# Routed experts walked block by block: one block of 64 slots per pass in place of pairs, tokens gathered once, put-back summed in PSUM, each expert matrix in one 2 MB transfer

## The reference

```python
def hierarchical_moe(h, w_gr, b_gr, w_er, b_er, w_gate, w_up, w_down):
    t = h.reshape(-1, d)                                   # 256 tokens x 1024
    g_sel = argmax(t @ w_gr + b_gr)                        # 1 of 8 groups
    top_v, top_i = top_k((t @ w_er + b_er)[group g_sel], 2)   # 2 of its 8 experts
    weights = g_gate * softmax(top_v)
    eid = g_sel * 8 + top_i                                # 512 assignments to 64 experts
    # the assignments, sorted by expert, are filled into blocks of one expert each
    hid = silu(xblk @ w_gate[e]) * (xblk @ w_up[e])        # 1024 -> 512, twice
    y = hid @ w_down[e]                                    # 512 -> 1024
    out = zeros.at[buf_tok].add(y * buf_w)                 # back to the tokens, weighted
```

## Time and profile before

| | us |
|---|---|
| runs (three) | 2862.37, 2856.97, 2859.93 |
| median | 2859.93 |
| span of the profiled execution (first to last instruction) | 2857.3 |
| median less that span (what lies around it) | 2.6 |
| first expert load issued | 2180.6 |
| last down matmuls of the experts end | about 2845.4 |
| first experts' matmul starts | 2193.45 |

### The profile page before, as it was taken

One profiled execution on the slowest core, in us unless ns is written; L12 is line 12 of the kernel. 1 busy time (PEld: TensorE's weight loads), 2 busy tenths in 40 slices (PEclk: granted clock), 3 DMA queues, 4 the chain that ended last, 5 costly groups with the idle time before them and its releaser, 6 DMA issues. The chain is left out here.

```text
span 2857.3 us, 42442 instructions
## 1 busy us (share of the span) xinstructions
PE 2778.7 (97%) x17857; PEld 2263.3 (79%) x17857; DVE 1517.0 (53%) x2889; ACT 479.1 (17%) x971; POOL 0.2 (0%) x4
## 2 busy tenths in 40 slices
PE   8999899999999999999999999999997999999998
PEld 8998799999988999888988998888895444443443
DVE  7768677687555775544345666466324322222232
ACT  1001410010043101122010022344101100101001
POOL 0000000000000000000000000000000000000000
PEclk9999999999999999999999999999998999999999
DMA  7544144464444553446544444454544999999996
GB/s 234 204 162 148 59 155 170 136 204 166 127 137 131 164 177 119 122 115 151 174 148 147 145 121 121 135 153 126 148 137 192 425 425 428 426 427 426 426 426 290
DMA packets 370397, 594.89 MB, mean 208 GB/s; under 512 B 15777, under 2 KB 327361, under 8 KB 347585
## 3 DMA queue, kind: packets, MB, share of 16 engines
q1 hardware_dynamic: 365440, 588.01, 58.4%
q10 hardware_dynamic: 4800, 4.63, 0.6%
HBM read 591.52 MB, written 1.08 MB: 207 GB/s over the span
## 5 line engine op out<-in xcount | busy, mean ns | idle before, releaser
L3246 PE MATMUL bank<-ring,wk 128*64 128x512 f32 x1408 | 313.6, 598 | 4.8 <-DMA ring<-in_w_expert_gate 4.8
L851 PE MATMUL bank<-hR,ring 128*128 128x128 f32 x2112 | 266.4, 276 | 4.0 <-DVE hR L427 4.0
L3246 PEld LDWEIGHTS bank<-ring,wk 128*64 128x64 f32 x1408 | 100.0, 138 | 211.5 <-issue 211.5
L851 PEld LDWEIGHTS bank<-hR,ring 128*128 128x128 f32 x2112 | 251.7, 193 | 4.9 <-DMA ring<-in_ffn_w_in 2.7
L3343 DVE TENSOR_TENSOR hT<-bank,hT 128x512 f32<-128x512 f32 x92 | 63.6, 691 | 312.5 <-PE bank L3233 310.1
L3272 PE MATMUL bank<-big,wk 128*64 128x512 f32 x352 | 155.8, 595 | 15.1 <-ACT wk L3303 15.1
L1171 PE MATMUL bank<-big,ring 128*128 128x128 f32 x1320 | 159.6, 275 | 0.0
L1171 PEld LDWEIGHTS bank<-big,ring 128*128 128x128 f32 x1320 | 153.5, 192 | 0.1
L740 PE MATMUL bank<-hR,ring 128*128 128x256 f32 x704 | 152.3, 379 | 0.0
L740 PEld LDWEIGHTS bank<-hR,ring 128*128 128x128 f32 x704 | 133.8, 190 | 18.2
L2276 PE MATMUL bank<-big,ring 128*128 128x256 f32 x640 | 141.0, 379 | 1.5 <-ACT big L2840 1.0
(11 more groups left out here) (454 smaller groups left out, 4718.3 us busy)
## 6 DMA issues: line engine op xcount, KB each, us to landing
ring<-in_ffn_w_in SPq DMA_DIRECT2D x88, 1024.0 KB
ring<-in_w_expert_gate SPq DMA_DIRECT2D x44, 2048.0 KB
ring<-in_w_expert_up SPq DMA_DIRECT2D x44, 2048.0 KB
ring<-in_w_in SPq DMA_DIRECT2D x96, 512.0 KB
big<-in_w_expert_down SPq DMA_DIRECT2D x44, 1024.0 KB
ring<-in_ffn_w_out SPq DMA_DIRECT2D x40, 1024.0 KB
ring<-in_w_up SPq DMA_DIRECT2D x22, 1024.0 KB
hR<-in_w_expert_down SPq DMA_DIRECT2D x22, 1024.0 KB
```

Source lines behind the costliest of these rows:

```text
L851: last = nc.tensor.matmul(k.bank[:, 2 * (n % 4) + p // 4, (p % 4) * P:(p % 4 + 1) * P], a[:, c, m * P:(m + 1) * P], b[:, c, :], start=c == ...
L3246: last = nc.tensor.matmul(k.bank[a:a + SLOTS, 2 + n, :], xg[:, c * P + a:c * P + a + SLOTS], self.weights(j, c, KC), start=c == 0, stop=c ...
```

## The change

The loop goes over single blocks and runs exactly as many times as there are blocks. Gate and up of one block now share a PSUM bank and the two column halves of the array; the two halves of the down product's columns do the same. All 512 assignments' tokens are gathered once, ahead of the loop, sorted by expert without gaps (`sorted_rows`, 8 x 576 columns); a block's 64 tokens are a window in it that starts at `k.first[block]`, which ScalarE copies out. The put-back matmuls add into four PSUM banks that hold the residual stream's sum over all blocks (`start=False`); these are cleared once ahead of the loop and added to the residual stream once behind it. Each matrix of a block has one place, `ring` slot 0 (gate), 1 (up) or 2 (down), and comes in one transfer of 2 MB. The residual rows are copied by ScalarE (in `TokenNorm`) and no longer by VectorE. The first constant's row is widened to 512 numbers. The core of the diff:

```diff
+    PIECES = 3
+    GU, TURN, DOWN = 7, (4, 6), 5
+    def arrived(self, eng, n, i):
+        sem, count = self.landing(n)
+        eng.wait_ge(sem, i * 16 + (count + 16))
+    def freed(self, i, n):
+        return i * self.PIECES + (self.u0 + NSLOT + n)
     def sp(self, sp):
         sp.wait_ge(self.route.eid_ready, 1)
+        with sp.Fori(0, self.blocks(sp)) as i:
+            e = sp.value_load(k.eid[0:1, bass.ds(i, 1)], min_val=0, max_val=NEXP - 1)
...
+            for n, w in enumerate((gate, up, down)):
+                sp.wait_ge(k.w_used, self.freed(i, n + 1 - self.PIECES))
+                sp.dma_start(self.piece(n), w).then_inc(self.landing(n)[0], 16)
+    def clear(self, pe):
...
+        for n in range(4):
+            nc.tensor.matmul(k.bank[:, n, :], self.w(self.GW, P), self.w(self.Y, 512), start=True, stop=True, ...)
+    def gather(self, pe):
...
+        for c in range(KC):
+            if c >= 3:
+                pe.wait_ge(self.xs_taken, c - 2)
+            for t in range(T):
+                last = nc.tensor.matmul(k.bank[:, 5 + c % 3, :], k.xn[:, t, c * P:(c + 1) * P], self.w(self.G + t * 512, 512), ...)
+            last.then_inc(self.xs_made, 1)
+    def put(self, pe, final=False):
...
+        for n in range(4):
+            r = slice((n % 2) * SLOTS, (n % 2 + 1) * SLOTS)
+            last = nc.tensor.matmul(k.bank[:, n, :], gw[r, (n // 2) * P:(n // 2 + 1) * P], y[r, :], start=False, stop=True, ...)
     def pe(self, pe):
+        with pe.Fori(0, n) as i:
+            pe.wait_ge(self.xg_ready, i + 1)
+            for m in range(2):
+                self.arrived(pe, m, i)
+            for c in range(KC):
+                for m in range(2):
+                    last = nc.tensor.matmul(k.bank[m * SLOTS:(m + 1) * SLOTS, self.GU, :], xg[:, c * SLOTS:(c + 1) * SLOTS],
+                                            self.piece(m)[:, c * 512:(c + 1) * 512], start=c == 0, stop=c == KC - 1)
+            last.then_inc(k.w_used, 2)
+            pe.wait_ge(self.y_taken, i + 1)
+            pe.wait_ge(self.gw_ready, i + 1)
+            self.put(pe)
+            pe.wait_ge(self.hid_ready, i + 1)
+            ... 4 transposes of 64x128 ...
+            pe.wait_ge(self.ht_taken, i + 1)
+            self.arrived(pe, 2, i)
+            for c in range(4):
+                for m in range(2):
+                    a = c * DM + m * 512
+                    last = nc.tensor.matmul(k.bank[m * SLOTS:(m + 1) * SLOTS, self.DOWN, :], ht[:, c * SLOTS:(c + 1) * SLOTS],
+                                            self.piece(2)[:, a:a + 512], start=c == 0, stop=c == 3)
+            last.then_inc(k.w_used, 1)
     def act(self, act, chain):
+        with act.Fori(0, self.blocks(act)) as i:
+            first = act.value_load(k.first[0:1, bass.ds(i + 1, 1)], min_val=0, max_val=2 * S)
+            act.wait_ge(k.w_used, self.freed(i, 2))
+            nc.scalar.activation(self.w(self.SI, 512)[SLOTS:P, :], k.bank[0:SLOTS, self.GU, :], ACT.Silu)...
+            nc.scalar.activation(self.window(), self.sorted_rows()[:, :, bass.ds(first, SLOTS)], ACT.Copy).then_inc(self.xg_ready, 1)
+            act.wait_ge(self.ht_ready, i + 1)
+            nc.scalar.activation(pair(self.w(self.HT, 256)), ..., ACT.Copy).then_inc(self.ht_taken, 1)
+            act.wait_ge(k.w_used, self.freed(i, 3))
+            nc.scalar.activation(self.w(self.Y, 512), k.bank[:, self.DOWN, :], ACT.Copy).then_inc(self.y_taken, 1)
     def dve(self, dve, chain):
+        with dve.Fori(0, n) as i:
+            ... up * gate in two halves of 64x256 (hid_ready), then the put-back matrix gw ...
```

More of the change, by code:

```diff
@@ L653, in act @@
         for n in range(4):
-            act.wait_ge(self.experts.put_taken, rounds * per + (4 + n + 1))
+            act.wait_ge(self.experts.x_summed, n + 1)
             nc.scalar.activation(k.wk[:, n * 512:(n + 1) * 512], self.quarter(k.x, n), ACT.Square, scale=1.0 / 32,
@@ L3173, in __init__, with landing, piece, sorted_rows @@
         self.route = route
[L3174 to L3193, removed]
+    def arrived(self, eng, n, i):
+        sem, count = self.landing(n)
+        eng.wait_ge(sem, i * 16 + (count + 16))
+    def landing(self, n):
+        return self.k.w_loaded[n], (self.u0 - n + NSLOT - 1) // NSLOT * UNIT_INC
+    def freed(self, i, n):
+        return i * self.PIECES + (self.u0 + NSLOT + n)
     def w(self, base, n):
         return self.k.wk[:, base:base + n]
+    def piece(self, n):
+        return self.k.ring[:, n, :]
+    def sorted_rows(self):
+        return self.w(self.XS, KC * self.WIDE).rearrange("p (c n) -> p c n", c=KC)
+    def window(self):
+        return self.w(self.XG, KC * SLOTS).rearrange("p (c n) -> p c n", c=KC)
     def sp(self, sp):
@@ L3200, in sp @@
         sp.wait_ge(self.route.eid_ready, 1)
[L3201 to L3215, removed]
+        with sp.Fori(0, self.blocks(sp)) as i:
+            e = sp.value_load(k.eid[0:1, bass.ds(i, 1)], min_val=0, max_val=NEXP - 1)
+            gate, up, down = (k.arg[name][0][bass.ds(e, 1), :, :].rearrange("e (p a) n -> p (e a n)", p=P)
+                              for name in ("w_expert_gate_3", "w_expert_up_3", "w_expert_down_3"))
+            for n, w in enumerate((gate, up, down)):
+                sp.wait_ge(k.w_used, self.freed(i, n + 1 - self.PIECES))
+                sp.dma_start(self.piece(n), w).then_inc(self.landing(n)[0], 16)
@@ new lines, in clear @@
+    def clear(self, pe):
+        k, nc = self.k, self.k.nc
+        pe.wait_ge(self.route.norm.xn_ready, 2)
+        pe.wait_ge(self.y_taken, 1)
+        pe.wait_ge(self.gw_ready, 1)
+        for n in range(4):
+            nc.tensor.matmul(k.bank[:, n, :], self.w(self.GW, P), self.w(self.Y, 512), start=True, stop=True,
+                             skip_group_check=True)
+    def gather(self, pe):
+        k, nc = self.k, self.k.nc
+        pe.wait_ge(self.route.norm.xn_ready, 1)
+        pe.wait_ge(self.sel_ready, 1)
+        for c in range(KC):
+            if c >= 3:
+                pe.wait_ge(self.xs_taken, c - 2)
+            for t in range(T):
+                last = nc.tensor.matmul(k.bank[:, 5 + c % 3, :], k.xn[:, t, c * P:(c + 1) * P], self.w(self.G + t * 512, 512),
+                                        start=t == 0, stop=t == 1)
+            last.then_inc(self.xs_made, 1)
@@ new lines, in take_sorted @@
+    def take_sorted(self, act):
+        k, nc = self.k, self.k.nc
+        for c in range(KC):
+            act.wait_ge(self.xs_made, c + 1)
+            nc.scalar.activation(self.sorted_rows()[:, c, 0:2 * S], k.bank[:, 5 + c % 3, :], ACT.Copy,
+                                 scale=k.p("norm_ffn_w_3 by row", c)).then_inc(self.xs_taken, 1)
+    def put(self, pe, final=False):
+        k, nc = self.k, self.k.nc
+        gw, y = self.w(self.GW, S), self.w(self.Y, 512)
+        for n in range(4):
+            r = slice((n % 2) * SLOTS, (n % 2 + 1) * SLOTS)
+            last = nc.tensor.matmul(k.bank[:, n, :], gw[r, (n // 2) * P:(n // 2 + 1) * P], y[r, :], start=False, stop=True,
+                                    skip_group_check=True)
+            if final:
+                last.then_inc(self.put_done, 1)
+        if not final:
+            last.then_inc(self.put_done, 1)
@@ L3217, in pe @@
     def pe(self, pe):
         k, nc = self.k, self.k.nc
-        def gather():
-            g = self.w(self.G, 256)
-            for c in range(KC):
[L3224 to L3260, removed]
+        ident = k.c("ident")
@@ L3265, in block @@
-            halves = [6 * s + 4, 6 * s + 5]
-            for j in halves:
-                pe.wait_ge(self.loaded(j), self.loads(j, i))
-            for h in range(2):
-                for c in range(4):
-                    for half, j in enumerate(halves):
-                        a = half * SLOTS
-                        last = nc.tensor.matmul(k.bank[a:a + SLOTS, 5 + h, :], ht[:, c * P + a:c * P + a + SLOTS],
-                                                self.weights(j, c, 4)[:, h * 512:(h + 1) * 512], start=c == 0, stop=c == 3)
-                        if h and c == 3:
-                            last.then_inc(k.w_used, 1)
@@ L3277, in pe @@
-        pe.sem_inc(self.put_taken, 4)
-        pe.wait_ge(self.route.norm.xn_ready, 1)
-        pe.wait_ge(self.sel_ready, 1)
-        gather()
-        pe.wait_ge(self.route.rows_taken, 2)
-        pe.wait_ge(self.route.eid_ready, 1)
-        n = self.rounds(pe)
-        with pe.Fori(0, n) as i:
-            for s in range(self.PAIRS):
-                block(i * self.PAIRS + s, s, i)
-        pe.wait_ge(self.y_taken, n * self.PAIRS + 1)
-        pe.wait_ge(self.gw_ready, n * self.PAIRS + 1)
-        pe.wait_ge(self.put_taken, n * (4 * self.PAIRS) + 4)
@@ L3293, in act @@
+        pe.wait_ge(self.y_taken, n + 1)
+        pe.wait_ge(self.gw_ready, n + 1)
+        self.put(pe, final=True)
     def act(self, act, chain):
         k, nc = self.k, self.k.nc
-        act.wait_ge(self.route.eid_ready, 1)
-        n = self.last = self.rounds(act)
```

(67 more changed lines are left out.)

122 lines of the change are left out of this document (62 added, 60 removed).

## The result

| | runs | median us | ratio to the kernel before, 95% interval |
|---|---|---|---|
| before (runs beside) | 2856.97 to 2862.37 | 2858.62 | |
| changed kernel | 3182.44 to 3186.57 | 3183.22 | 1.1131 [1.1118, 1.1145] |

The change made the kernel 325 us (11.3%) slower; 3180 was forecast, with a range of 3070 to 3225. The profiled execution took 3182.85 us, with a span of 3181.0.

What follows compares the result with a forecast made beforehand. TensorE and the weight transfers were both taken as full in the expert loop, 14.75 us a block. Forecast: 2212 + 42 x 22.54 + 19.1 = 3177.8 us of span, 3180 us with what lies around it; range 3070 to 3225.

Steps and rivals of the forecast that it cites:

- The ring of waits: Expert loop: with one place per matrix, gate and up loads and their matmuls take turns; 22.54 us a block against 14.75.
- From the end of gate-and-up to the next: Expert loop: 0.16 us until SP issues the load, then 12.88 us until the matmul that needs both matrices.
- The row taken: Profile of the kernel before, loop's first load: issued at 2180.57, TensorE starts at 2193.45, giving 12.88 us.
- The clock: TensorE in each block: a stop halves the clock for 5.05 us, costing 2.5; gate-and-up take 9.5 us instead of 7.04.
- Gate-and-up of block 0: Loop start: they wait for the sorted tokens, start at about 2204 us (2199 to 2217) and end at about 2212.
- the tail: After the last gate-and-up: 7.7 us to the last down matmul, then 11.9 less 0.4 to the span's end; 19.1 together.
- What lies beside: Put-back, SiLU, transposes, down in each block: end 6.8 to 8.6 us after gate-and-up, hidden under the 13.0 us load, costing nothing.
- 4 to 6 us in which TensorE waits: Expected trace sign: before each gate-and-up group TensorE waits this long for a gate or up transfer.
- The count of blocks: Expert loop: 43 real blocks instead of 44, one block of padding less, 14.75 us at the present pace.
- Rival A: Expert loop: same waits but TensorE stays at full clock, 20.08 us a block, 3075 us; chance 0.16.
- rival C: Expert loop: SP gets a block ahead, transfers stay gapless, 14.75 us a block, 2851 us, 0.3% faster; chance 0.02.
- B's longer half clock: Expert loop: gate-and-up run at half clock throughout, 14.1 us, 27.1 a block, 3378 us; chance 0.08.

Runs made afterwards that it cites:

- the run with down queued right behind: Changed kernel with two places for down alone, gate and up keeping one, block 0 ahead of a loop over pairs of blocks; 3172.27 us.
- the run with the clock kept: Changed kernel with nine idle matmuls of 128x384 behind each block's down matmuls, filling TensorE's stop; 3094.25 us.

## Why the prediction was right, point by point

- **The ring of waits** is the cause. It is in the chain of waits, and giving each matrix a second place takes the whole loss away, while the same loop with a second place for down alone stays at 3172 us.
- **From the end of gate-and-up to the next:** forecast 0.16 + 12.88 = 13.04, measured 13.35 on the mean of 42. The row taken had further loads queued behind the pair, and here there are none until the down matrix 6.4 us later. That this makes the 0.3 us is not shown; the run with down queued right behind has 13.19. The Trainium skill's figure (DMA: Bandwidth & Descriptors, Anatomy of one DMA), measured on GpSimd's path, 2.0 us and the bytes, an estimate of 11.6, is farther off.
- **The clock:** forecast 9.5 us for gate-and-up from three half-clock stretches, measured 9.31, the mean of 8.42 to 10.10 us. Three stretches met the mean of so wide a spread within 0.2 us, in which there is some luck. That a half clock follows in every block is right: in the loops of the changed kernel and of the experiments each stop of 4.15 to 7.05 us that was not filled had a gate-and-up of 8.4 us or more behind it.
- **The two errors nearly cancel, by luck:** + 0.31 - 0.19 a block, 42 times 0.12 = 5 us. Gate-and-up of block 0 end at 2211.1 (2212 forecast), the tail is 17.5 (19.1), and around the span lie 1.9 (2.6): - 0.9 - 1.6 - 0.7. Of 3180 this makes 3182, the profiled 3182.85.
- **What lies beside:** the down matmuls end 6.5 us after gate-and-up, just below the forecast's 6.8 to 8.6. The low end had the put-back's row halves beside each other, and so they run (last section); the transposes took 0.34 us and not 0.45. TensorE's stop is so 6.8 us on the mean and not 4.4 to 6.2, and the sign "4 to 6 us in which TensorE waits" was missed. These steps were off the path, as said, and cost nothing. That nothing in the trace before shows row halves was a misreading. The scores of an attention stage there are matmuls of 64 rows, half of them in the upper and half in the lower rows of the array: four of 256 columns take 0.61 us, where those with 128 rows take 7.07 / 32 = 0.22 us each, 0.88 for four:

```profile
1755.14 0.61 PE L1896 MATMUL bank<-wk 64*128 64x256 f32 x4
...
1756.44 7.07 PE L1531 MATMUL bank<-hR,ring 128*128 128x256 f32 x32
```

- **The count of blocks** is 43. Rival A (the clock holds, 3075) describes the run with the clock kept (3094); rival C (gapless, 2851) that with two places (2841). Neither describes the change as it stands, and B's longer half clock did not come.

## What to carry to other kernels

Count the places of each buffer before the engines' work: where a load must wait for the reader of its own place, load and reader add up, however full either was before. Here the load of gate and up and the matmuls on them added up to 20.4 us a block even at full clock, against 14.7. And price what a new stop does to the clock: the run with the clock kept puts 89 of the 325 us, about a quarter, on the half-clock matmuls, and most of the rest is the wait.

## What the runs showed of the hardware that was not expected

The put-back's four matmuls with 64 rows each, alternating between the upper and lower half of the array, take 1.99 us, against 3.63 with 128 rows; the changed kernel's timeline:

```profile
2211.02 1.99 PE L3261 MATMUL bank<-wk 64*128 64x512 f32 x8
```

A pair of 2 MB loads into an empty queue took 13.35 us on the mean (13.02 to 13.59) from the end of the matmuls that free its places to the matmuls that read it, 0.16 less in the run with down queued behind, and 0.53 less when issued as four of 1 MB; none of the three was explained. Nor was it explained why behind nearly equal stops of 6.5 to 7.05 us gate-and-up took now 8.42 and now 10.10 us.
